# Shift rows of the last norm by a rank-two product on TensorE, weight row applied ahead of the moments

## The reference

```python
def layer_norm(x, g, b):
    mu = mean(x); var = mean((x - mu)**2)
    return (x - mu) * rsqrt(var + 1e-5) * g + b

h = x * (1 + sc2) + sh2
gate, up = split(h @ w_gu, 2)
f = (silu(gate) * up) @ w_down          # w_down: 5632 x 2048
y = layer_norm(ALPHA * x + g2 * f, ln2_g, ln2_b)
```

## Time and profile before

| | |
|---|---|
| runs | 2701.7, 2700.77, 2698.55 us; median 2700.77 |
| profiled execution | 2699.8 us, of which the span is 2698.0 us |
| TensorE busy | 2635.9 us (98% of the span) |
| VectorE busy | 1421.8 us (53%) |
| ScalarE busy | 897.9 us (33%) |
| GpSimd busy | 644.7 us (24%) |
| mean granted clock of TensorE | 0.994 |

### The profile page before, as it was taken

How to read it: one execution, slowest core, us unless ns; L and a number is a source line. 1 busy time by engine, 2 the same in 40 slices (tenths; PEclk the granted TensorE clock), 3 DMA queues, 4 the chain that set the end, 5 groups by cost and what they waited for, 6 DMA issues and landing times.

```text
span 2698.0 us, 37412 instructions
## 1 busy us (share of the span) xinstructions
PE 2635.9 (98%) x16040; PEld 2353.1 (87%) x16040; DVE 1421.8 (53%) x1681; ACT 897.9 (33%) x940; POOL 644.7 (24%) x217
## 2 busy tenths in 40 slices
PE   5999999999999999999999999999999999999997
PEld 3787878797988879999999999999999888888886
DVE  5323332356575458555565545554556444444578
ACT  4333333333311154333333333333333333333243
POOL 0000000000000001434443444344433333333440
PEclk8999999999999999999999999999999999999999
DMA  9775757423463142333233223322334646454586
GB/s 378 281 267 208 275 201 272 161 78 107 178 219 125 61 157 84 106 109 98 84 109 109 92 90 109 109 89 92 109 109 148 239 175 214 175 215 168 193 275 226
DMA packets 182024, 438.11 MB, mean 162 GB/s; under 512 B 10060, under 2 KB 30932, under 8 KB 175716
## 3 DMA queue, kind: packets, MB, share of 16 engines
q1 hardware_dynamic: 179556, 430.48, 45.8%
q10 hardware_dynamic: 2304, 5.24, 0.5%
HBM read 401.83 MB, written 33.85 MB: 161 GB/s over the span
## 4 chain that ended last, share of the span: by engine, by line
PE 73%; POOL 8%; DVE 7%; DMA 6%; issue 3%; ACT 2%; SPq 0%; POOLq 0%; ACTq 0%; DVEq 0%
PE ps L2357 7%; PE ps L2358 7%; PE ps L2359 7%; PE ps L2434 7%; PE ps L2435 7%; PE ps L2436 7%; PE ps L2107 5%; PE ps L2109 5%; PE ps L2108 5%; DMA raw_w<-w_gu_b 4%; PE ps L2087 3%; PE ps L2306 3%; PE ps L2305 3%; PE ps L2304 3%; POOL raw_w L981 2%
## 5 line engine op out<-in xcount | busy, mean ns | idle before, releaser
L1703 DVE TENSOR_TENSOR w_lo<-raw_w,w_hi 128x1024 fp32r<-128x1024 f32 x264 | 336.3, 1275 | 296.8 <-ACT w_hi L1247 294.0
L1247 ACT ACTIVATE w_hi<-raw_w 128x1024 fp32r<-128x1024 f32 x264 | 270.0, 1054 | 599.5 <-POOL raw_w L987 378.6
L2357 PE MATMUL ps<-x_hi,w_hi 128*128 128x320 f32 x1408 | 435.8, 310 | 3.6 <-DVE w_lo L1703 2.0
L2359 PE MATMUL ps<-x_hi,w_lo 128*128 128x320 f32 x1408 | 435.1, 309 | 0.0
L2358 PE MATMUL ps<-x_lo,w_hi 128*128 128x320 f32 x1408 | 435.0, 309 | 0.0
L978 POOL TENSOR_TENSOR low<-raw_w 128x1024 f32<-128x1024 f32 x41 | 104.2, 2543 | 1085.0 <-DMA raw_w<-w_gu_b 1031.4
L1848 DVE TENSOR_TENSOR x_lo<-low,x_hi 128x2560 fp32r<-128x2560 f32 (+2 forms) x55 | 223.4, 4062 | 261.4 <-ACT x_hi L1340 261.4
L2434 PE MATMUL ps<-w_hi,x_hi 128*128 128x512 f32 x880 | 342.8, 390 | 2.0 <-POOL w_lo L993 0.8
L2435 PE MATMUL ps<-w_lo,x_hi 128*128 128x512 f32 x880 | 342.4, 389 | 0.0
L2436 PE MATMUL ps<-w_hi,x_lo 128*128 128x512 f32 x880 | 342.3, 389 | 0.0
L2357 PE MATMUL ps<-low_r,w_hi 128*128 128x320 f32 x1072 | 331.9, 310 | 0.8 <-DVE low_r L1789 0.7
(11 more groups left out here) (241 smaller groups left out, 4262.3 us busy)
## 6 DMA issues: line engine op xcount, KB each, us to landing
raw_w<-w_gu_b SPq DMA_DIRECT2D x180, 512.0 KB, 5.6
low<-w_ada SPq DMA_DIRECT2D x68, 1024.0 KB, 6.9
raw_w<-w_down SPq DMA_DIRECT2D x50, 1024.0 KB, 5.1
low<-hidden_scratch SPq DMA_DIRECT2D x33, 1280.0 KB, 6.1
raw_w<-w_in_b SPq DMA_DIRECT2D x33, 1024.0 KB, 9.1
x_raw<-w_ada SPq DMA_DIRECT2D x25, 1024.0 KB, 14.4
raw_w<-w_out SPq DMA_DIRECT2D x16, 1024.0 KB, 5.1
hidden_scratch<-high SPq DMA_DIRECT2D x44, 320.0 KB, 5.8
```

The source lines that it names most:

```text
L1247: nc.scalar.activation(weight(0, w), src, ACT.Copy).then_inc(prod_hi, 1)
L1703: nc.vector.tensor_tensor(weight(1, n), src, weight(0, n).bitcast(F32), ALU.subtract).then_inc(prod_split, 1)
L2357: mm(out, wh, version(v, 0, k), start=first and k == 0, stop=False)
L2359: ins = mm(out, wl, version(v, 0, k), start=False, stop=last and k == HK - 1)
```

## The change

For tiles 3 and 4 the norm is written as x * g * r + (-mean * r) * g + 1 * b, with r = 1/std.

- *Weight row ahead of the moments.* Blocks 0 to 2 of tiles 3 and 4 are multiplied by ln2_g on VectorE (`early_gain`), two passes of 512 columns in each of the last three of units 33 to 43. Their statistics were taken before. Block 3 is multiplied by GpSimd, once the moments of the tile are there (semaphore `late_gain`).
- *Shift rows.* VectorE forms -mean * r, a column (`shift_of`). TensorE turns it into a row by a product with the identity, ScalarE copies the row to SBUF beside a row of ones (`mean_ones`), and TensorE multiplies these two rows of 128 by the two rows ln2_g and ln2_b (`shift_gain`, loaded by one small DMA), in float32, four products of 512 columns for a tile. The result is in PSUM.
- *One pass.* `shifted_piece` on VectorE is then x * r + PSUM for a half tile, in place of the two passes.
- The reciprocal of tile 3 and its `shift_of` stand between the two passes of the evacuation of tile 4.

```diff
+            if j == LAST_B + 3:                                   # SP
+                sp.wait_ge(down_used, LAST_B)
+                sp.dma_start(shift_gain, rows[4:6, :].rearrange("r (k c) -> r k c", k=KT)
+                             ).then_inc(tail_pair_in, 16)
...
+        pool.wait_ge(down_used, LAST_B)                           # GpSimd, at its end
+        nc.gpsimd.memset(x_spare[0:2, 0:2, 2 * P:3 * P], 1.0).then_inc(late_gain, 1)
+        for t in range(TAIL, TT):
+            pool.wait_ge(moments, TT + t + 1)
+            blk = folded_tile(t)[:, 6:8]
+            nc.gpsimd.tensor_tensor(blk, blk, ln2_row[0][:, 6:8], ALU.mult).then_inc(late_gain, 1)
...
         for t in range(TAIL, TT):                                 # ScalarE
             tail_root(t)
+            act.wait_ge(late_gain, 1)
+            act.wait_ge(mean_turned, t - TAIL + 1)
+            nc.scalar.activation(mean_ones(t)[0:1], ps[0:1, TURN_BANK[t - TAIL], 0:P],
+                                 ACT.Copy).then_inc(mean_row, 1)
...
             link(nc.vector.tensor_tensor(acc, acc, high[:, at:at + 512], ALU.mult))
+            if nb == 3 and t == TT - 1:
+                rstd_of(t - 1)
+                shift_of(t - 1)
             nc.vector.scalar_tensor_tensor(blk, blk, ALPHA, acc, ALU.mult, ALU.add).then_inc(down_evac, 1)
...
+        def shift_of(t):
+            dve.wait_ge(late_root, t + 1 + t - TAIL)
+            nc.vector.scalar_tensor_tensor(mv(t, 3), mv(t, 0), -1.0, mv(t, 2), ALU.mult,
+                                           ALU.mult).then_inc(late_root, 1)
+        def early_gain(nb):
+            dve.wait_ge(tail_rows_in, 32)
+            for t in range(TAIL, TT):
+                dve.wait_ge(down_evac, TT * nb + t + 1)
+                blk = folded_tile(t)[:, 2 * nb:2 * nb + 2]
+                ins = nc.vector.tensor_tensor(blk, blk, ln2_row[0][:, 2 * nb:2 * nb + 2], ALU.mult)
+            link(ins)
+        def shifted_piece(t, i):
+            tile = u_acc[:, t, 1024 * i:1024 * i + 1024]
+            at = 512 * SHIFT_BANK[t - TAIL][i]
+            dve.wait_ge(shift_filled, 2 * (t - TAIL) + i + 1)
+            if i:
+                dve.wait_ge(late_gain, 2 + t - TAIL)
+            dve.wait_ge(late_root, t + 2 + t - TAIL)
+            nc.vector.scalar_tensor_tensor(tile, tile, mv(t, 2), flat_ps[:, at:at + 1024], ALU.mult,
+                                           ALU.add).then_inc(y_done, 1)
...
                 ready_rows(nb, g)
+                if nb == 3 and g >= N_DG - 3:
+                    early_gain(g - N_DG + 3)
...
-        for t in range(TAIL, TT):
-            rstd_of(t)
-            for i in range(2):
-                gain_piece(t, i)
-                bias_piece(t, i)
+        shifted_piece(TAIL, 0)
+        rstd_of(TAIL + 1)
+        shift_of(TAIL + 1)
+        shifted_piece(TAIL, 1)
+        for i in range(2):
+            shifted_piece(TAIL + 1, i)
...
+        pe.wait_ge(tail_pair_in, 16)                              # TensorE, at its end
+        for t in range(TAIL, TT):
+            pe.wait_ge(late_root, t + 2 + t - TAIL)
+            mm(ps[0:1, TURN_BANK[t - TAIL], 0:P], mv(t, 3), ident, start=True, stop=True).then_inc(mean_turned, 1)
+            pe.wait_ge(mean_row, t - TAIL + 1)
+            for i in range(2):
+                if t > TAIL and i:
+                    pe.wait_ge(y_done, 2 * TAIL + 1)
+                for h in range(2):
+                    k = 8 * i + 4 * h
+                    bank = ps[:, SHIFT_BANK[t - TAIL][i] + h, :].rearrange("p (k c) -> p k c", c=P)
+                    ins = mm(bank, mean_ones(t), shift_gain[:, k:k + 4], start=True, stop=True)
+                ins.then_inc(shift_filled, 1)
```

More of the change, by code:

```diff
@@ L619, in backbone @@
     y_out = sem("y_out")
+    tail_pair_in = sem("tail_pair_in")
+    mean_turned = sem("mean_turned")
+    mean_row = sem("mean_row")
+    shift_filled = sem("shift_filled")
+    late_gain = sem("late_gain")
     dve_step = sem("dve_step")
@@ L641, in backbone @@
     ln2_row = [x_rows[:, 8 * i:8 * i + 8, TAIL * P:T] for i in range(2)]
+    shift_gain = x_rows[0:2, 0:KT, 2 * P:3 * P]
+    TURN_BANK = (7, 0)
+    SHIFT_BANK = ((3, 5), (1, 3))
     def folded_tile(t):
@@ L649, in backbone, with mean_ones @@
     x_spare = x_raw[:, KT * T:2 * KT * T].rearrange("p (k c) -> p k c", c=T)
+    def mean_ones(t):
+        return x_spare[0:2, t - TAIL, 2 * P:3 * P]
     def down_slot(j):
```

## The result

The changed kernel took 2706.57 us (median of 12 runs, 2705.07 to 2711.91), the kernel before 2700.48 us in the same comparison (12 runs, 2698.55 to 2704.34). The ratio is 1.0024 with a 95% interval of 1.0017 to 1.0032: 4.6 to 8.6 us slower. Forecast were 2698.4 us and a range of 2695.6 to 2701.2; the result lies outside it, on the slower side, to which the prediction gave 0.02.

What follows compares the result with a forecast made beforehand. The end was taken as a VectorE chain of 12.6 us; +1.33 us for added passes and -3.69 at the end gave -2.36, a profiled 2697.4, and 1.0 up to the median, 2698.4 us; range 2695.6 to 2701.2.

Steps and rivals of the forecast that it cites:

- the price of the shift rows: TensorE's float32 products at the end: 1.09 us for a pair of 512 columns, 0.90 for the next.
- -3.69: The end, from TensorE's last product to VectorE's last pass: last pass at 2691.24 in place of 2694.93, 3.69 us earlier.
- The clock between the tiles: Rival, chance 0.18: TensorE at 1.2 GHz for tile 4's shift rows; end gains 2.11 us, time 2700.0 us.
- The slower rival: Rival, chance 0.04: float32 products take twice the time for both tiles; +0.35 us, 2701.1 us.
- The third pair: Last two added weight-row passes on VectorE, uncovered: unit 47 and all behind it 1.33 us late, bounds 0 to 2.0.
- Pairs 1 and 2: First four added weight-row passes on VectorE, claimed hidden in its waits of 1.69 and 2.84 us: no cost.
- caught behind GpSimd: Rival, chance 0.07: one added VectorE pass waits for GpSimd's subtraction, 0.66 us on the path; -1.70, 2699.1 us.
- Between the evacuation passes of tile 4: Reciprocal and small product on VectorE there: 1.06 us between the large passes against 0.73 without, 0.33 us added.
- The small product: VectorE's product of two SBUF columns at 2683.33: left open whether it waits for GpSimd, 0 to 0.1 us.
- GpSimd's block 3: GpSimd's weight-row multiplication at the end: 1.15 us for each tile, 4.6 us available, so no cost.
- The copy: ScalarE's copy of the turned row from PSUM in the end's chain: 0.27 us.
- if the clock reads 0.50 ahead of tile 4's products: Sign against the forecast, which expected TensorE to stay at 2.4 GHz through the end.

Runs made afterwards that it cites:

- a_padded_fed: Changed kernel with ten unread 128-row products in TensorE's waits at the end and the two-row products zero-padded to 128 rows; ratio to the kernel before 1.0000.
- a_fed: Changed kernel with ten unread 128-row products put into TensorE's waits at the end, shift-row products still of two rows; ratio to the kernel before 1.0017.
- a_moved: Changed kernel with the third pair of weight-row passes moved into VectorE's waits in units 49 and 50; ratio to the kernel before 1.0015.
- a_rounded_two: Changed kernel with two float32r products, high and low part, for each float32 shift-row product; GpSimd makes the low part; ratio to the kernel before 1.0014.
- a_high_moved: Changed kernel with one float32r product of rounded values per float32 one, low parts left out, third pair moved to VectorE's later waits; ratio to before 0.9991.
- a_rounded_moved: Changed kernel with two float32r products for each float32 one and the third pair moved to units 49 and 50; ratio to the kernel before 1.0012.

## Why the prediction was wrong

**The step that failed** is the price of the shift rows: "the eight of 45.85, which lie four side by side and so two deep, take 1.06 us; the four of 154.12, of 1280 columns in all, take 1.34, which gives a pace of 0.44 us for 512 columns. I take 1.09 for a pair and 0.90 for the next". The rows were right, what I counted in them was not. `x8` is four products, side by side and so one deep, and `x4` is two: the trace before, by source line, has for line 2148 (ns min/median/max, first and last start in us, forms)

```profile
L2148 PE MATMUL ps<-low x4: 269/430/693, 154.1 to 155.2; 33*128 33x512 f32 x2, 33*128 33x128 f32 x2
```

and the code issues one product of 512 columns and one of 128 there, 640 columns in 1.34 us and not 1280. A product of 512 columns is two records of 0.43 us, so a pair fills its half in 1.93 us and the next 1.72 later at 2.4 GHz (a_padded_fed), and 3.8 and 3.4 us at 1.2 GHz (VectorE's passes of tile 4 start 3.8 us behind the first product, and 3.41 apart). With the clock held this step alone turns -3.69 into -1.08: 2.6 us. With the 5.15 us of the clock (below) it makes up the whole 7.8 us between the forecast end and the measured one, +4.07.

The Trainium skill, "FP8 and Floating Point Precision", section "TensorE Precision Notes", has four passes through the array for true float32, by my estimate 0.85 us for 512 columns. The trace agrees: 2 x 0.43 = 0.86. The prediction had this rule and set it aside since "The 1280 columns in 1.34 us disagree with it"; that sentence was the miscount.

**The clock between the tiles** was a rival with 0.18, worth 1.6 us (an end shorter by 2.11 us in place of 3.69) for products of half the length. It came true, and dearer, because the products are twice as long, the turn at half clock takes 0.59 us and not 0.46, and the fall did not wait for the gap between the tiles. I had argued that the clock would stay since TensorE "does some products in between"; a_fed shows that products of two rows with TensorE always busy didn't hold it, a_padded_fed that those of 128 rows did. The rows of before say the same: there TensorE does nothing behind its last product, which ends at 2682.32, and the clock falls 4.7 us later; after it falls 4.2 us behind that product and in a_moved 2.5 us, with the two-row products in between. So it falls no later with them than with nothing. The fall costs 16.68 - 11.53 = 5.15 us.

**The slower rival** had the mechanism (products of twice the length, the second tile turned only after the first is filled) and 2701.1 us, without the clock's fall. It had 0.04. The long products alone leave the time near that of before (a_padded_fed, 1.0000), and by my estimate so does the clock alone: in a_rounded_two, whose eight products for tile 3 take about what was assumed, the clock falls between the tiles and the end is 1.55 us shorter than before, against 1.1 us more in the units. Together they make it slower. I had priced each as a case of its own and never the two together.

**The third pair** was forecast at +1.33 us and measured at +1.11, with TensorE waiting for VectorE as written, but only half of it ahead of unit 47 (idle 1.09 us, forecast about 1.9); the other half lies at units 45 and 46. Pairs 1 and 2 cost nothing: ScalarE is let go at 2605.85, 2614.01 and 2622.17, 8.16 us apart as before (2605.42, 2613.58, 2621.74), and behind them the units take 61.69 us with all three pairs and 61.67 with the third alone. No pass was caught behind GpSimd. It went the other way round at pair 1: GpSimd's subtraction took 5.08 us in place of 4.60, and `hid_rest` behind it 5.19 in place of 4.71, both under cover.

**The rest held.** Between the evacuation passes of tile 4 lie 1.06 us, as in the earlier trace rows. The small product waits for GpSimd, which the prediction had left open at 0 to 0.1 us: it is recorded for 0.21 us in place of 0.16 and ends at 2685.04, 0.02 behind the end of GpSimd's pass (2683.76 + 1.26), and in a_high_moved for 0.28 us and ends 0.01 behind. Otherwise GpSimd's block 3, 1.26 us, forecast 1.15, is waited for by nobody:

```profile
2683.76 1.26 POOL L1017 TENSOR_TENSOR low<-low,x_raw 128x512 f32<-128x512 f32 x1 [61.32 <-DVE perm L2032]
```

The copy takes 0.27 us, the store 3.06. Of what the prediction named as proof against it, "if the clock reads 0.50 ahead of tile 4's products" is what came.

**What stays open.** The parts of the profiled execution give +5.2 us, the medians +6.1 with an interval from 4.6 to 8.6; since a_moved and after show the fall at different moments of the same end, one profile can't say more. What exactly keeps the clock up, rows in use or something that goes with them, was tried only with 2 and 128 rows.

## What to carry to other kernels

Before a pace is taken from a group of matmuls in a trace, count the products in the code and divide: a float32 product is two records, and the price of a chain that VectorE waits for doubles with them. Work that goes onto TensorE behind its last dense stage must be priced at both clocks, because thin products there may not hold the upper one, and two slips that can meet in one chain need a case for their sum. And compare parts between the same two events: 1.1 us in the units is plain there and invisible in the medians.

## What the runs showed of the hardware that was not expected

- A float32 product is recorded as two matmuls, each about 0.43 us for 512 columns at 2.4 GHz (3.70 us for eight) and 0.85 at 1.2 GHz (7.19 for eight). A float32r product is one, 1.11 to 1.19 us for four.
- The granted clock fell to 0.50 in the midst of products of two rows (they run back to back from 2685.98, the fall is at 2688.10), and with feeding as well (2687.53); with 128 rows, 126 of them zeros, and feeding it stayed at 1.00, and with 128 rows alone it fell at 2688.75 and came back at 2692.17.
- In the midst of the dense units the clock fell too, behind 3.29 us in which TensorE waited (a_rounded_moved, 0.50 from 2661.62 to 2665.03); behind 2.46 us it did not (a_rounded_two).
- GpSimd's subtraction of 2048 columns takes 4.84 us on 2 partitions, as 4.60 on 128, and VectorE's pass that starts within it lasts 5.08 us in place of 1.22. The Trainium skill, "SBUF — State Buffer", section "SBUF: two separate sides", says that VectorE and GpSimd share a pair of ports, which is an exclusive lock for the whole instruction. The rows agree, and add that few partitions don't shorten it.
